# A two-part transformer kernel: the hand-off order between its matmul stream and its side work is written anew

## The reference, cut to what matters

```python
# first_block, for each of 2 layers (modulated by ada_w, a matrix-vector product of c):
out_a = sliding_window_attention(rope(rmsnorm(aq)), rope(rmsnorm(ak)), av, sinks)   # 8 heads
out_b = rmsnorm(hgrn2_chunked(bq, log_f, bv)) * silu(bg)                            # 4 heads
out_c = rmsnorm(gated_delta_chunked(cq, ck, cv, beta, g)) * silu(cg)                # triangular solve
x = x + gate * (concat([out_a, out_b, out_c]) @ w_out)
x = x + gate * ((silu(h @ w_gate) * (h @ w_up)) @ w_down)
# second_block, for each of 2 layers:
proj = x @ w_in_2[layer]                      # 1024 -> 14400 columns
y_ssd   = ssd_branch(silu(dwconv5(xbc)), dt, ...)  # scan in chunks, both directions, 32 heads
y_diff  = softmax(q1 k1) v - lam * softmax(q2 k2) v
y_cross = cross_attention(cq, mem_kv)
merged  = gates[0] * (y_ssd @ w0) + gates[1] * (y_diff @ w1) + gates[2] * (y_cross @ w2)
x = layernorm(alpha * x + merged @ w_out_2[layer])
```

## Time and profile before

| | |
|---|---|
| median of 3 runs | 3949.34 us (3945.07 to 3956.91) |
| the profiled execution | 3945.07 us |
| its span, first to last instruction | 3943.2 us |
| PE busy | 3771.9 us, 96% |
| PE weight loads busy | 3093.5 us, 78% |
| DVE busy | 2621.1 us, 66% |
| ACT busy | 1563.8 us, 40% |
| POOL busy | 182.0 us, 5% |
| DMA, mean | 115 GB/s |
| mean granted TensorE clock | 0.980 of full speed |

### The profile page before, as it was taken

How to read it: one execution, slowest core, us unless ns; L and a number is a source line. 1 busy time by engine, 2 the same in 40 slices (tenths; PEclk the granted TensorE clock), 3 DMA queues, 4 the chain that set the end, 5 groups by cost and what they waited for, 6 DMA issues and landing times.

```text
span 3943.2 us, 49348 instructions
## 1 busy us (share of the span) xinstructions
PE 3771.9 (96%) x19428; PEld 3093.5 (78%) x19428; DVE 2621.1 (66%) x4158; ACT 1563.8 (40%) x2633; POOL 182.0 (5%) x335
## 2 busy tenths in 40 slices
...
GB/s 240 178 22 71 86 172 208 188 116 91 71 38 60 110 95 89 104 113 127 160 163 160 72 97 80 67 116 131 75 153 142 158 169 88 94 95 53 81 139 107
DMA packets 226871, 451.59 MB, mean 115 GB/s; under 512 B 18560, under 2 KB 63648, under 8 KB 224592
## 3 DMA queue, kind: packets, MB, share of 16 engines
...
HBM read 412.45 MB, written 35.93 MB: 114 GB/s over the span
## 4 chain that ended last, share of the span: by engine, by line
PE 76%; DVE 15%; ACT 4%; DMA 2%; issue 2%; SPq 0%; POOL 0%; DVEq 0%; ACTq 0%; POOLq 0%
PE ps L608 59%; PE ps L151 11%; PE ps L162 4%; DVE arena L173 3%; DVE spl L173 3%; DVE arena L188 3%; ACT arena L247 2%; PE ps L157 1%; DVE sm L194 1%; DVE X L173 1%; PE ps L859 1%; ACT sph L247 1%; DMA arena<-cumd 1%; DVE arena L224 1%; DVE arena L180 1%
## 5 line engine op out<-in xcount | busy, mean ns | idle before, releaser
L173 DVE TENSOR_TENSOR spl<-ring,sph 128x1024 fp32r<-128x1024 f32 (+3 forms) x556 | 650.5, 1178 | 686.8 <-ACT sph L247 686.1
L247 ACT ACTIVATE sph<-ring 128x1024 fp32r<-128x1024 f32 (+3 forms) x556 | 558.6, 1019 | 732.9 <-PE ps L608 698.6
L608 PE MATMUL ps<-sph,HTh 128*128 128x512 f32 (+2 forms) x1632 | 635.9, 390 | 8.7 <-DVE HTl L173 5.0
L608 PE MATMUL ps<-spl,HTh 128*128 128x512 f32 (+2 forms) x1632 | 601.8, 369 | 0.0
L608 PE MATMUL ps<-sph,HTl 128*128 128x512 f32 (+2 forms) x1632 | 600.7, 368 | 0.0
L247 ACT ACTIVATE arena<-ps 128x512 f32<-128x512 f32 (+2 forms) x572 | 315.6, 564 | 683.2 <-PE ps L608 403.6
L608 PE MATMUL ps<-HTh,sph 128*128 128x512 f32 x1360 | 537.7, 395 | 11.2 <-ACT X L247 10.5
L608 PE MATMUL ps<-HTl,sph 128*128 128x512 f32 x1360 | 530.6, 390 | 0.0
L608 PE MATMUL ps<-HTh,spl 128*128 128x512 f32 x1360 | 530.6, 390 | 0.0
L608 PE MATMUL ps<-sph 128*128 128x512 f32 x992 | 397.9, 401 | 5.1 <-DVE spl L173 5.1
L608 PE MATMUL ps<-sph,spl 128*128 128x512 f32 x992 | 387.8, 391 | 0.0
(11 more groups left out here) (224 smaller groups left out, 4917.7 us busy)
## 6 DMA issues: line engine op xcount, KB each, us to landing
...
arena<-cumd POOLq DMA_DIRECT2D x128, 256.0 KB, 4.0
...
```

Of the source, the lines that this page charges most:

```text
L173: self.e.tensor_tensor(o, a, b, op).then_inc(*self.done.up())
L247: self.e.activation(o, a, f, **kw).then_inc(*self.done.up())
L608: ins = pe.e.matmul(o, l, r, start=k0 == 0 and i == 0 and not b.pairs, stop=k0 + b.ks == b.kt and i == 3 * b.ks - 1 and (c0 > 0 or not b.p ...
```

## The change

Only the strings of `SCORES` change, for the four stages mix 0, mix 1, proj 0 and proj 1. Each string holds as many steps of each stream as before, in another order; no step gains or loses an instruction.

```diff
     ('mix', 0):
-        "14Mt3MtM2t10MtM2a7Ma4Ma2MhMaMc5Mh3Mc2Mc5Ma3Mca9Ma3Mah8Ma3Mc2MaMaMahMc2MaMahMc2Mc4Mc2gaha2gh3gaha2gag"
+        "7Mt2Mt4Mt2Mt2Mt10MaMa10MaMaMah8Mc3Mc4MhMc3MaMaMa2MaMc10Mh9MahMaMac3M2aMhMc2MaMh2McMc2Mca2M2ga2gh3gah"
...
     ('mix', 1):
-        "24Ma7Ma2M2aMh2Mah2c2MacMacM3a3M3a2Ma7Mh4Mc4Mhac2MaMa3Maca2McMaMaMchMh4M2gh5gha2gag2a4gag2agag2agag2a"
+        "24MaMaMa2Ma4MaMh4McaMha2cMca2Mca3Ma3Ma2MaMhMa4MaMc4Ma2Ma2Ma2MaM2hcMaMcMcaMah5M2gh5gah2gag2a4gag2agag"
...
     ('proj', 0):
-        "19Mc3Mcs5Mcdsc3MdMd5Md4Mc4McMc2McMdMdMcd2M2cdMd2cd6Mc3McMd3Md2McMd3Md2Mcd3Md2M2d2c2d3MsdMcMc2Md3Md2M"
+        "18Md2M2s2M2d2McMcMcMd2Mc2Md5M2c5Md3Mc2dc3Md5Mc2dMc2dM2dcMc2Mcd2Mc3Md14M2c3Mc2McMdcMdsMdsd3c2MdMcdM2s"
...
     ('proj', 1):
-        "Mr10Mr2M2r11Mdcd4Ms3Md3Md2Mc2McM2d3MscMcMdc2Mcdc6McMdcd2c4McMd5MdcMc5Md7M2c3MdcM2d3McdMcMdMc2Ms2M2dM"
+        "2r5Mr9Mr5MdMs3Mc7Mc3Mdc6MdMc2MdMcM2c2MdMc2Mc3Md3MdMd2Mdc2Md2c2M2dMd3Mc3M2c5Md3M2d2csc2MdMc3Mc3MdMdsM"
...
```

More of the change, by code:

```diff
@@ L49 @@
     ('mix', 0):
-        "14Mt3MtM2t10MtM2a7Ma4Ma2MhMaMc5Mh3Mc2Mc5Ma3Mca9Ma3Mah8Ma3Mc2MaMaMahMc2MaMahMc2Mc4Mc2gaha2gh3gaha2gag"
-        "agag2agagagag2agag2ag3a3g2a3gahmihtimhim2Mihi3MihMi5M2hihi2Mih3MiMh2iM2iMihiMih2iMi2h2Mi2MhMihihMhih"
-        "Mh2iMihMh4MiM2iM2i2M2iMiM2i4Mb21M",
+        "7Mt2Mt4Mt2Mt2Mt10MaMa10MaMaMah8Mc3Mc4MhMc3MaMaMa2MaMc10Mh9MahMaMac3M2aMhMc2MaMh2McMc2Mca2M2ga2gh3gah"
+        "a2gagagag2agagag2agagag2a2g3a2g3a2ghgmihimhim4Mhi3Mh2iMhiMiMiMhiMihi4MhMit2Mhihi2MhihMi2MiMhiMiMhiMh"
@@ L53 @@
+        "Mih3ihihi2MhiMhihiM2iMi2MiMiMi2M2i4Mb21M",
     ('mix', 1):
-        "24Ma7Ma2M2aMh2Mah2c2MacMacM3a3M3a2Ma7Mh4Mc4Mhac2MaMa3Maca2McMaMaMchMh4M2gh5gha2gag2a4gag2agag2agag2a"
-        "g2ag2agm3gihimhim3Mhi2Mi2MhiMhihiMiMhihi3MiMhiMiMihMiMhi2h2MhMi3MhiMh2iM3ihihihiMhi2hMi2M2iM2i2M2i2M"
-        "iMiMi11Mb17M",
+        "24MaMaMa2Ma4MaMh4McaMha2cMca2Mca3Ma3Ma2MaMhMa4MaMc4Ma2Ma2Ma2MaM2hcMaMcMcaMah5M2gh5gah2gag2a4gag2agag"
+        "ag2ag2agag2a3gagmihimhim4Mi2MhMiMhihiMihiMihiMi2MihiMiMhiMhihiMhihMhMi3MiMihi3MhihihihiMih3M2i2Mi2hM"
@@ L57 @@
+        "iMi2MiM2i3M2ib25M",
     ('proj', 0):
-        "19Mc3Mcs5Mcdsc3MdMd5Md4Mc4McMc2McMdMdMcd2M2cdMd2cd6Mc3McMd3Md2McMd3Md2Mcd3Md2M2d2c2d3MsdMcMc2Md3Md2M"
[L59 to L62, removed]
@@ L63 @@
-        "g7Mgt8MtMtM3t3Mt2MtMt8MtMt2M3t4Mt4M3t5MtMt8M5t15M3t9Mt12Mt3Mg4Mt5Mt3Mt8MfM2f5Mf2Mf2Mf2MfMfMf2MfMfMf"
-        "2MfMfMfMfMf2Mf3MfMfMfMnf2Mf3Mf3Mn4Mf5Mf2Mn2Mf4Mf2MfMf2Mfn3MfnM2f2MfMfMfMfMnxn2Mxy2xnMyx2yxny2nMyMx8M"
-        "y4M2z5M2z4Mz25M2m8Ms7M2mMm29M",
-    ('proj', 1):
-        "Mr10Mr2M2r11Mdcd4Ms3Md3Md2Mc2McM2d3MscMcMdc2Mcdc6McMdcd2c4McMd5MdcMc5Md7M2c3MdcM2d3McdMcMdMc2Ms2M2dM"
[L68 to L74, removed]
+        "18Md2M2s2M2d2McMcMcMd2Mc2Md5M2c5Md3Mc2dc3Md5Mc2dMc2dM2dcMc2Mcd2Mc3Md14M2c3Mc2McMdcMdsMdsd3c2MdMcdM2s"
@@ new lines @@
+        "5Md5McsMdc2Md6McdcMd4Mc2MdMc2dMc2Md2Mcs2MsdMscdsMdMd4Ms2McMdMdMs3MdMc2McMd2s2Mc3McdMs2Md6Mcs3McMcdsc"
+        "dc2ds3Mc2Md3McMsdsc2Mc3Mdc4Ms4cMdMcMcscdMd2Md3M3dsMsdcMc2MsdM2c2Mc2Mc2dMdcs2M2sMsMs3MsMs4M2s2M2s3MsM"
+        "sMp3MsM2pMsM2psp3Ms3Mp2spsMp4Mps2MpMpM3ps2p2M2spMpMspMsMspMs2Ms2Mp2Mp2Msp2Mpsp2s5M3p2sMp3Mp2sMpMspMp"
+        "M2s2p2MsMspMpMsM2p2s2pMpM2p5Mpg3p2M4pM2p2MpMpM2pMpMpM2p2M3p2MgMpgM3p2MpM2p3MpM4pM3p4Mg19Mg4Mg4MgMg5M"
+        "g4MtMt2MtMt4Mg2MtM3tMt2Mt2M2t3Mt2Mt2M2t3Mt5Mt5MtMt2Mt2Mt2Mt3MtMt5Mt4Mt2Mt3Mt30M3t6Mt7Mf2M2f2MfMf5MfM"
```

10 lines of the change are left out of this document (added).

## The result

The kernel after takes 3987.91 us, the median of four runs (3979.33 to 3990.88); beside it the kernel before took 3949.48 (3945.07 to 3956.91). The ratio is 1.0094, with a 95% interval of 1.0082 to 1.0107: 38 us slower, where +7.6 was forecast and 3980 was the upper end of the range. The profiled executions differ by as much, 3982.99 against 3945.07.

The account below looks back on a forecast made before the run. PE's matmul stream was taken as the bound; -6.6 - 1.5 - 6.1 + 9.8 + 6 + 4 + 2 = +7.6 us gave 3952.7 against the profiled execution, 3957 against the median, range 3933 to 3980.

Parts of the forecast that it names:

- the exposed chain: Proj 0, ssd steps 0 and 1 both at 20: PE idles through the DVE and ACT chain, +9.8 us, bounds 5.6 to 11.0.
- the clock's part: Proj 0, behind the wait at ssd steps 0 and 1: matmuls at half clock, 2.9 us of the +9.8.
- drain of the table loads: Proj 0, ACT: about 1.38 us extra per table load would make the +9.8 term +12.6; left out of the sum.
- the dense stretch of proj 0: Proj 0, 1900 to 2260 us: bunched ssd, pass and conv steps delay main's low halves, +4 us, bounds 0 to +12.
- rival B: Dense stretch: DVE's backlog decides, three waits of 3.24 us with half clock, 18.4 us instead of 4, total 3971; chance 0.25.
- both holes on DVE: Mix 0: angles steps fill DVE's idle 2.12 and 3.48 us, shortening PE's wait at hgrn step 2; -6.6 us with clock.
- the wait of conv1: Proj 1: PE's 3.24 us wait for DVE at conv1's fourth step goes with its half clock, -6.1 us, bounds -6.1 to 0.
- its loads for the ring keep their place relative to main: SP's queue: the ring's loads keep their place relative to main, counted at nothing.
- the diff pairs: Proj 0: three more pairs of diff steps with no main step between, 2.1 us of waiting each, +6 us, bounds 0 to 8.
- The wait of 10.48 us: Mix 1: PE's wait for ACT stays; the rest of the stage gains 1.5 us, between 0 and 3.

Follow-up runs that it names:

- e11: Kernel before with ssd step 1 of proj 0 moved from position 27 to 22, next to step 0; single run, main step 60 late by 9.8 us.
- e8: Kernel before with four angles steps of mix 0 placed as in the kernel after and proj 1's fourth conv1 step moved from 34 to 37; ratio 0.9993.
- e4: Kernel after with the first four rest steps of proj 1 (finishing and saving x) back at positions 1, 11, 13 and 13; ratio 1.0087.
- e3: Kernel after with proj 0's conv, ssd, pass, gated and turns steps from position 180 on placed as before; loss over main steps 190 to 290 is 1.0 us.
- e9: Kernel before with proj 0's conv, ssd, pass, gated and turns steps from position 180 on placed as in the kernel after; ratio 1.0045, 18 us slower.
- e5: Kernel after with DVE's low halves of the weights in proj 0 computed for half of their columns only; ratio 1.0071.
- e13: Kernel after with 41 ssd and pass steps of proj 0 put at least two main steps behind their partners, two pairs left; 25.5 us lost, main steps 190 to 290.
- e14: Kernel after with 14 ssd and pass steps of proj 0 put at least one main step behind their partners; 23.9 us lost between main steps 190 and 290.
- e16: Kernel after with the two-main-step distance carried through in proj 0, 50 steps moved; 24.9 us lost between main steps 190 and 290.
- e18: Kernel before with only the two-main-step distance carried through in proj 0, 33 steps moved; loses 4.4 us between main steps 180 and 320.
- e15: Kernel before with the two-main-step distance in proj 0 (32 steps), diff, dnorm and cross steps as after, proj 1's fourth conv1 step at 37; ratio 1.0038.

## Why the prediction was wrong, step by step

**Right: the exposed chain.** +9.8 for `ssd` steps 0 and 1 side by side; 9.8 in e11, 11.4 in the kernel after, where PE also waits 0.87 us ahead of step 0. The rows of the chain gave its length. That the clock's part fits e11 to the tenth is partly luck: it was taken from another wait, and in the kernel after it is 5.1 us (last section). No drain of the table loads is in it, as ACT's row had said.

**The step that failed: the dense stretch of proj 0.** The mechanism was named, and was rival B, but the term was +4 with a bound of 12, and it is 22.7 between main steps 190 and 290, 23.3 from 60 to 440. Of these 23.3, 15.2 are more idle time of PE and 5.1 the lower clock. (From 190 to 290 the idle time is 12.7 more and the clock the same 5.1; the rest is mostly 18 side matmuls more that now stand in this stretch, and 290 to 440 gets 2.7 us shorter.) The bound was argued from DVE's 14% slack and from the fact that PE was idle there for only 2.3 us. Both say how well the old order fitted, not how much another can lose. Slack does not cover: in the kernel after DVE is idle for 34 of the 216 us between main steps 190 and 290, 16%, and PE waits for it all the same. Rival B's own picture, three long waits of 3.24 us with half clock, does not fit either: the longest are 3.11 and 2.93 us, with nine shorter ones above 0.3 us.

**Failed: both holes on DVE turned into gains.** Mix 0 was to gain 6.6 us and gained nothing (e8: wait 6.90 with the holes filled, 100 us ahead of it). The sum carried 5.6 us of freed time past some 60 main steps, over slack that I had counted myself as 8.4 us and put down as a mere bound. The lower end of that term, 0, was the answer. In the kernel after this wait is shorter, 3.24, but 4.76 us are spent nine us earlier, so the two are longer together.

**Failed: the wait of conv1.** It went, as forecast, and its 6.1 us did not come back: e8 shows the next wait two main steps on. In the kernel after a new wait of 5.21 us for a weight transfer came with the earlier save of x, a move that the prediction counted at nothing ("its loads for the ring keep their place relative to main"): the loads did, the 2 MB store beside them did not. e4 shows that the wait hangs on the place of these steps. Proj 1 was to be 4.1 us shorter and is 3.2 longer.

**Too high: the diff pairs.** +6 was forecast for them; PE waits 1.0 us more there, the longest of the waits for ACT in the L151 rows being 1.31 us, not 2.1. The stretch still got 1.7 us shorter: a wait of 2.72 us for a transfer behind it, and 1.7 us that the lower clock behind it cost, which no part of the prediction looked at, are gone.

**Mix 1: the wait right, the gain not.** The wait of 10.48 us is 10.47. The stage was to be 1.5 us shorter; it is 2.4 us longer here and 5.7 to 10.0 in the other traces with this order, at the lower clock shown above.

Of the miss of 30 us, 19 are the dense stretch, 7 proj 1, 7 mix 0, 4 mix 1 and 2 the chain, and -8 diff and -1 ahead of mix 0. This holds for these two traces; in the others with the mix stages of the kernel after, mix 1 has a larger part. What stays open is a rule for the dense stretch. Shown: its order alone makes the waits (e3, e9), and an accumulated backlog of low halves does not (e5). Argued only: a wait is made of what stands on DVE just ahead of the result. Distance to the partner step does not predict them (e13, e14, e16 to e18). Why e15's runs spread as they do is open too, and so is the lower clock in mix 1.
